# Gathers under way at the phase ends, inputs brought a phase early, and a merge that takes one operand after the other

## The reference

```python
h = rms_norm(x, n_mix_pre) * (1 + sc1) + sh1          # sc, sh, g: from the conditioning vector
bg, cg, hin, q, k, v, r, ga, gb, alow = split(h @ w_in)
branch_a = (bg * conv3(cg * hin)) @ w_proj_a
branch_b = (rms_norm(gated_linear_attention(q, k, v)) * silu(r)) @ w_proj_b
m = (sigmoid(ga) * branch_a + sigmoid(gb) * branch_b) @ w_out
x = x + g1 * rms_norm(m, n_mix_post)
h = rms_norm(x, n_ffn_pre) * (1 + sc2) + sh2
# PEER: 8 heads, each takes the 16 best of 128*128 experts by two sets of 128 sub-keys
s = (h @ wq) . subkeys; top 16 of each half, of the 256 sums the top 16 -> expert, gate = softmax
act = gelu(u_tab[expert] . h)                          # 128 rows of u per token
y = sum(gate * act * v_tab[expert])                    # 128 rows of v per token
x = x + g2 * rms_norm(y, n_ffn_post)
```

## Time and profile before

| | |
|---|---|
| runs | 4400.0, 4410.25, 4410.38 us |
| profiled execution, its own time | 4404.23 us |
| its span | 4402.1 us |
| busy | PE 3206.2 us (73%), DVE 2480.9 (56%), POOL 1645.8 (37%), ACT 804.7 (18%) |
| DMA | 1359.01 MB, mean 309 GB/s; gathers (queue q0) 1140.92 MB, other loads and stores (q1) 215.09 MB |
| part 0's phases | about 695 to 1174 us, gathers from 1080 us |
| part 1's phases | 1174 to 2171 us |
| part 2's phases | 2171 to 3370 us |
| last phase | 3370 to 4402 us |

### The profile page before, as it was taken

One profiled execution on the slowest core, in us unless ns is written; L12 is line 12 of the kernel. 1 busy time (PEld: TensorE's weight loads), 2 busy tenths in 40 slices (PEclk: granted clock), 3 DMA queues, 4 the chain that ended last, 5 costly groups with the idle time before them and its releaser, 6 DMA issues. The chain is left out here.

```text
span 4402.1 us, 46784 instructions
## 1 busy us (share of the span) xinstructions
PE 3206.2 (73%) x15781; PEld 1734.2 (39%) x15781; DVE 2480.9 (56%) x7734; ACT 804.7 (18%) x1299; POOL 1645.8 (37%) x1380
## 2 busy tenths in 40 slices
PE   5999997775597776766688666677665666677676
PEld 2998896754164542431155333144111111111111
DVE  2435554138764546777665554677775555555555
ACT  4223323342123112210014111211000010000000
POOL 2111104524255543543255444354333333333332
PEclk8999998977798986977789888698666666666666
DMA  8011003424799989989899999999899999999998
GB/s 339 26 60 60 31 30 129 127 98 145 292 373 370 364 354 359 378 346 364 322 383 410 360 358 361 384 412 364 356 399 361 412 415 404 411 415 404 415 413 345
DMA packets 225975, 1359.01 MB, mean 309 GB/s; under 512 B 29286, under 2 KB 38406, under 8 KB 83532
## 3 DMA queue, kind: packets, MB, share of 16 engines
q0 software_dynamic: 156672, 1140.92, 64.3%
q1 hardware_dynamic: 69068, 215.09, 13.4%
HBM read 1322.56 MB, written 33.35 MB: 308 GB/s over the span
## 5 line engine op out<-in xcount | busy, mean ns | idle before, releaser
L1083 DVE CUSTOM_DVE_ANT_0 peer_uv<-peer_uv,all_PS 128x512 f32<-128x512 f32 x2176 | 1435.4, 685 | 1140.3 <-PE all_PS L1021 585.5
L1021 PE MATMUL all_PS<-peer_hT,peer_sel 96*128 96x512 bf16 x2176 | 972.8, 463 | 949.3 <-DVE peer_halves L1083 799.0
L1004 POOL DMA_INDIRECT peer_uv<-in_uv,peer_idx x1088 | 1041.5, 957 | 1600.3 <-PE all_PS L1041 1198.8
L1021 PEld LDWEIGHTS all_PS<-peer_hT,peer_sel 96*128 96x128 bf16 x2176 | 205.0, 101 | 1776.3 <-DVE peer_halves L1083 1291.7
L1041 PE MATMUL all_PS<-peer_uv,peer_zw 128*32 128x512 f32 x4352 | 835.0, 869 | 1.5 <-DVE peer_zw L1103 1.5
L888 POOL TENSOR_TENSOR flow_w_lo<-flow_w,flow_w_hi 128x1024 fp32r<-128x1024 f32 (+1 forms) x204 | 460.4, 2262 | 541.1 <-ACT flow_w_hi L881 537.3
L1057 ACT ACTIVATE peer_ge<-peer_pre 128x4 f32<-128x4 f32 x272 | 56.1, 206 | 2121.4 <-DVE peer_pre L1089 1955.9
L1041 PEld LDWEIGHTS all_PS<-peer_uv,peer_zw 128*32 128x32 f32 x4352 | 154.0, 142 | 423.8 <-issue 422.0
L908 PE MATMUL all_PS<-mix_h_hi,flow_w_hi 128*128 128x384 f32 (+1 forms) x672 | 281.7, 419 | 31.6 <-POOL flow_w_lo L888 31.6
L881 ACT ACTIVATE flow_w_hi<-flow_w 128x1024 fp32r<-128x1024 f32 (+1 forms) x204 | 203.6, 1004 | 327.3 <-PE all_PS L910 134.9
L910 PE MATMUL all_PS<-mix_h_hi,flow_w_lo 128*128 128x384 f32 (+1 forms) x672 | 224.6, 334 | 0.0
(11 more groups left out here) (294 smaller groups left out, 4679.6 us busy)
## 6 DMA issues: line engine op xcount, KB each, us to landing
cond_w<-in_w_ada SPq DMA_DIRECT2D x12, 2048.0 KB, 11.8
flow_w<-in_w_gate_ab SPq DMA_DIRECT2D x48, 512.0 KB
flow_w<-in_w_query SPq DMA_DIRECT2D x48, 512.0 KB
flow_w<-in_w_conv SPq DMA_DIRECT2D x36, 512.0 KB
peer_uv<-in_uv,peer_idx POOLq DMA_INDIRECT x1088
gla_w<-in_w_heads SPq DMA_DIRECT2D x24, 512.0 KB, 3.9
flow_w<-in_w_proj_b SPq DMA_DIRECT2D x24, 512.0 KB
flow_w<-in_w_out SPq DMA_DIRECT2D x24, 512.0 KB
```

The costliest lines, as they stand in the source:

```text
L1004: self.nc.gpsimd.indirect_dma_start(out=self.uv[:, n % self.NUV, :], out_offset=None, in_=self.A["uv"], in_offset=bass.IndirectOffsetOnAxi ...
L1021: nc.tensor.matmul(PS[:, f, :], self.sel[:, c:c + 1].broadcast_to([3 * GR, P]), self.hT[:, g % self.NH, f * 512:(f + 1) * 512], start=True ...
L1083: nc.vector.tensor_tensor_reduce(part, part, PS[:, f, :], 1.0, 0.0, ALU.mult, ALU.add, self.halves[:, d, f, e:e + 1]).then_inc(M["dotted"], 1)
```

## The change

- `Gather.fetch` gets a third argument. With it POOL goes on to `upto + 8` (`FULL` = `NUV - 2`) and not to `upto + 4`. Every phase ends with `gat.fetch(pool, hi, True)` behind its loop; in norm and pick that call stands alone for all of POOL's gathers.
- The marks are rounded so that each hi is 2 modulo 4: part 0's pick takes 26 tokens and not 24, part 1 ends at 318 and part 2 at 702 and not at 320 and 704. So the sum of the last full group is issued by the phase's last spread, and of ten buffers eight are free.
- `Early`: tiles on the other side of SBUF that outlive a phase. The h of a part's mix is brought in the middle of the pick before it (`bring_h`); norm's lines, `pick` and x rows are brought in out. The taps and the bias of the convolution are loaded once, for part 0.
- In mix, merge and out ACT and DVE take the gather turns of `before()` first and split afterwards.
- merge takes all eight products of a (4 chunks each) and then all eight of o (8 chunks each), where it took them in turn; the stream of weights is ordered so, too. o is split at steps 3, 4, 5 and 6 of the loop, and the sums of the two come in steps 8 to 15.
- norm's scratch row lies in the tile of the key lists.

```diff
+    FULL = NUV - 2
-    def fetch(self, pool, upto):
+    def fetch(self, pool, upto, full=False):
-        for n in self.steps("pool", upto + self.AHEAD if upto else 0):
+        assert not full or upto in (0, T) or upto % BT == 2
+        for n in self.steps("pool", upto + (self.FULL if full else self.AHEAD) if upto else 0):
...
+class Early:
+    def __init__(self, nc, sems, tag, tiles):
+        self.room = Scope(nc, tag)
+        self.tiles = [self.room.twin(q, shape, "right") if twin else (self.room.sb(q, shape, side="right"), None)
+                      for q, shape, twin in tiles]
+        self.sems = sems
+    def free(self):
+        self.room.tensors.close()
+def bring_h(sp, A, part, brought):
+    for g in range(2):
+        sp.dma_start(brought.tiles[0][0][:, 4 * g:4 * g + 4], A["h1"][part.index, :, 4 * g:4 * g + 4, 0:part.n]).then_inc(brought.sems[g], 16)
...
 # mix_phase
-            h.fetch(sp)
-            for dst, src in ((taps, A["conv_w"]), (cbias, A["conv_b"]), (past, A["conv_state"])):
-                sp.dma_start(dst[:], src).then_inc(small_in, 16)
+            if part.index == 0:
+                bring_h(sp, A, part, brought)
+                for dst, src in ((taps, A["conv_w"]), (cbias, A["conv_b"]), (past, A["conv_state"])):
+                    sp.dma_start(dst[:], src).then_inc(small_in, 16)
+            gat.fetch(pool, hi, True)          # also behind the loops of merge, out and keys; alone in norm and pick
+            gat.gelu(act, turns.before())      # mix, merge and out alike
             h.make_high(nc, act)
-            gat.gelu(act, turns.before())
+            gat.dots(dve, turns.before())
             h.make_low(nc, dve)
-            gat.dots(dve, turns.before())
...
 # merge_phase
+        O_AT = (3, 4, 5, 6)
-                w.product(nc, pe, w0 + j, bank(j), (a, o)[j % 2], lambda k, nk: gat.spread(pe, turns.within(j, k, nk)))
+                w.product(nc, pe, w0 + j, bank(j), (a, o)[j // KD], lambda k, nk: gat.spread(pe, turns.within(j, k, nk)))
-            o.make_high(nc, act)
+                if j in O_AT:
+                    o.make_high(nc, act, O_AT.index(j))
-                d, q = divmod(j, 2)
+                q, d = divmod(j, KD)
...
 # out_phase, SP
+            for q in range(3):
+                sp.dma_start(lines[q * GR:q * GR + NC, :], A["rows"][q]).then_inc(brought.sems[0], 16)
+            sp.dma_start(pick[:, :], A["line_pick"]).then_inc(brought.sems[0], 16)
...
+                if 0 < j <= nt:
+                    i, u = j - 1, part.tiles[j - 1]
+                    sp.dma_start(x[0:part.rows[i], i, :], A["x_rows"][u, 0:part.rows[i], :]).then_inc(brought.sems[1 + i], 16)
...
 # pick_phase, SP
+                if j == NJ // 2 and following:
+                    bring_h(sp, A, following, brought)
...
 # hybrid_decoder
-                        marks = [0, 0, 0, 0, 0, 0, 24]
+                        marks = [0, 0, 0, 0, 0, 0, 26]
-                        span = gat.before[part.tiles[0]] - lo
-                        marks = [lo + span * sum(SHARES[:i]) // sum(SHARES) for i in range(len(SHARES) + 1)]
+                        span = gat.before[part.tiles[0]] - 2 - lo
+                        marks = [lo + span * sum(SHARES[:i]) // sum(SHARES) // BT * BT for i in range(len(SHARES) + 1)]
```

More of the change, by code:

```diff
@@ L916, with __init__ @@
 class Halves:
-    def __init__(self, sc, tag, chunks, n, group, source=None, twin=None):
+    def __init__(self, sc, tag, chunks, n, group, source=None, twin=None, landed=None):
         self.groups, self.group, self.source = chunks // group, group, source
@@ L922, in __init__ @@
         self.hi = sc.sb(f"{tag}_hi", [P, chunks, n], F32R)
-        self.landed = [sc.sem(f"{tag}_in{g}") for g in range(self.groups)] if source else None
+        self.landed = landed or ([sc.sem(f"{tag}_in{g}") for g in range(self.groups)] if source else None)
         self.high, self.low = sc.sem(f"{tag}_high"), sc.sem(f"{tag}_low")
@@ L1149, in mix_phase @@
         PS = G["PS"]
-        h = Halves(sc, "h", KD, n, 4, lambda g: A["h1"][part.index, :, 4 * g:4 * g + 4, 0:n])
+        h = Halves(sc, "h", KD, n, 4, twin=brought.tiles[0], landed=brought.sems)
         NJ, NCONV = 3 * CC + 2 * KD, 3 * CC
@@ L1342, in _ @@
         def _(sp):
+            lines, pick, x = (q for q, _ in brought.tiles)
+            for q in range(3):
+                sp.dma_start(lines[q * GR:q * GR + NC, :], A["rows"][q]).then_inc(brought.sems[0], 16)
+            sp.dma_start(pick[:, :], A["line_pick"]).then_inc(brought.sems[0], 16)
             gat.turn(sp, turns.before())
@@ L1383, in _ @@
         def _(act):
+            gat.gelu(act, turns.before())
             x.make_high(nc, act)
-            gat.gelu(act, turns.before())
             for j in range(NJ):
@@ L1396, in _, with norm_phase @@
         def _(dve):
+            gat.dots(dve, turns.before())
             x.make_low(nc, dve)
-            gat.dots(dve, turns.before())
             for j in range(NJ):
                 gat.dots(dve, turns.upto(j))
-def norm_phase(nc, A, G, part, gat, m_rows, h, lo, hi):
+def norm_phase(nc, A, G, part, gat, m_rows, brought, junk, h, lo, hi):
     with Scope(nc, f"norm{part.index}") as sc:
@@ L1407, in norm_phase @@
         R = part.rows
-        x = sc.sb("x", [P, nt, D])
-        lines, pick = sc.sb("lines", [3 * GR, D]), sc.sb("pick", [3 * GR, P + TAIL])
-        junk = sc.sb("junk", [P, D])
+        lines, pick, x = (q for q, _ in brought.tiles)
+        lines_in, x_in = brought.sems[0], brought.sems[1:]
         ss, root = sc.sb("ss", [P, 2, nt]), sc.sb("root", [P, 2, nt])
         assert not part.samples or part.index == 0
-        lines_in, row_mm, squared, logged, rooted, gated, x2_done, gained, h2_done, t_mm, high = (sc.sem(q) for q in (
-            "lines_in row_mm squared logged rooted gated x2_done gained h2_done t_mm high").split())
-        x_in, x2_saved = ([sc.sem(f"{q}{i}") for i in range(nt)] for q in ("x_in", "x2_saved"))
+        row_mm, squared, logged, rooted, gated, x2_done, gained, h2_done, t_mm, high = (sc.sem(q) for q in (
+            "row_mm squared logged rooted gated x2_done gained h2_done t_mm high").split())
+        x2_saved = [sc.sem(f"x2_saved{i}") for i in range(nt)]
         block = sc.block()
@@ L1426, in _ @@
         def _(sp):
[L1427 to L1431, removed]
             gat.turn(sp, turns.before())
@@ L1441, in _ @@
         def _(pool):
-            gat.fetch(pool, turns.before())
-            for j in range(NJ):
-                gat.fetch(pool, turns.upto(j))
+            gat.fetch(pool, hi, True)
         @block.tensor
@@ L1703, in lows, with pick_phase @@
         return 2 * self.tiles
[L1706 removed]
+def pick_phase(nc, A, G, part, gat, best, place, following, brought, lo, hi):
     with Scope(nc, f"pick{part.index}") as sc:
@@ L1734, in _ @@
                 gat.turn(sp, upto(j))
+                if j == NJ // 2 and following:
+                    bring_h(sp, A, following, brought)
         @block.gpsimd
         def _(pool):
-            for j in range(NJ):
-                if j >= early:
-                    gat.fetch(pool, upto(j))
+            gat.fetch(pool, hi, True)
         @block.tensor
@@ L2015, in hybrid_decoder @@
                     with Scope(nc, f"mid{part.index}") as mid:
-                        spare = mid.sb("spare", [P, len(part.tiles) * D])[:, :]
+                        nt = len(part.tiles)
+                        spare = mid.sb("spare", [P, nt * D])[:, :]
                         m_rows = spare.rearrange("p (t d) -> p t d", d=D)
+                        norm_in = [mid.sem(f"norm_in{i}") for i in range(nt + 1)]
                         with Scope(nc, f"join{part.index}") as join:
```

70 lines of the change are left out of this document (44 added, 26 removed).

## The result

| | before | after |
|---|---|---|
| median (lowest to highest), us | 4407.39 (4400.0 to 4410.38), 4 runs | 4511.85 (4510.58 to 4517.03), 4 runs |
| profiled execution's span, us | 4402.1 | 4510.0 |
| ratio after / before | | 1.0242, 95% interval 1.0224 to 1.0260 |

The kernel became 104 us slower; 4504 was forecast. The page's DMA slices after, to hold against the earlier trace rows: many nines of the parts' stretches have become eights, and one a six; those of the last phase stand.

The account below looks back on a forecast made before the run. DMA was taken as the bound: bytes over 411 GB/s plus its idle time at the barriers. 4404.2 + 97 - 4 = 4497 for the profiled execution, 6 us under the runs' median, so 4504; range 4430 to 4550 us.

Parts of the forecast that it names:

- POOL's drain waits for landing; the barrier for the drain: Phase ends: POOL's drain returns only once its gathers landed; the last four gathers add 10.2 us to it.
- rival A: Drain not held by the landing, so eight gathers run through the barrier: faster, about -75, 4335 us; chance 10%.
- No buffer free until the first sum: Behind the barriers: eight buffers full, no gather until the next sum; idle 153.8 us against 56.4, cost 97 us.
- Idle ahead stays: Ahead of the barriers: DMA idle time from the last packet to the open barrier stays, only shifted by the longer queue.
- a DMA share above 0.8 ahead of the barriers: Sign of the forecast: no engine busy for some 20 us before each barrier while DMA share there rises above 0.8.
- Part 0, -4: Part 0, without gathers: norm and merge starts lose short waits, between 0 and 8 us, 4 taken as gain.
- Marks, 0 (-3 to +3): Rounded marks, smaller tiles and taps loaded once: taken as 0, bounds -3 and +3.
- Order of merge, 0 (-5 to +25): Merge, all of a then all of o: up to 3 us in 8 steps of two merges; 0 taken, bounds -5 to +25.
- cross-check: Counting engine time: 13 barriers each open 10.2 us later, 133, less 38 given back at the starts: +95.
- Starts: Phase starts in the check by engine time: merge 2 x 7, mix 2 x 5, norm 2 x 7, 38 us given back.
- Rival B: No difference: +56 behind barriers, up to 45 us regained later in the phases by eight tokens in hand; 4417, chance 8%.
- Rival C: Slower still: second group of four late in mix and keys, merge's o half bound by PE; +25 to +45, 4540; chance 12%.

Follow-up runs that it names:

- experiment 1: Changed kernel with POOL's fetch at a phase's end reaching 0, 4 or 6 tokens beyond hi, where it was 8: 4446.94, 4392.04 and 4454.47 us.
- (3): Six phases' barriers of semaphores alone, no POOL drain: changed kernel 4310.36 us, with fetch to hi + 4 only 4319.46 us; kernel before 4347.18 us.
- experiment 5: Kernel before with only the rounded marks, gathers to hi + 4 at the ends as before: 4418.96 us, ratio 1.0045.
- open barriers: Changed kernel with the barriers at the six phases' ends made of semaphores alone and POOL not draining there: 4310.36 us, ratio 0.9804.
- experiment 4: Changed kernel without POOL's drain at the six phases' ends: merge in turn again 4325.69 us; splitting ahead of the gather turns again 4308.48 us.
- Experiment 2: Kernel before with only the rounded marks and the fetch to hi + 8 at the phase ends: 4547.02 us, ratio 1.0343.

## Why the prediction was right

By its own steps:

- **POOL's drain waits for landing; the barrier for the drain.** Right: 2.8 us for each gather more (experiment 1), gone with the drain (3), and the drains end 1.5 to 4.4 us behind the last gather packet. What rival A took for its condition, a drain that the landing does not hold, is not what happened.
- **No buffer free until the first sum.** Right: 148 us idle behind the barriers, 154 forecast; +92 over the kernel before, +97 forecast. By phase, both parts, in us idle of 30 (forecast, part 1, part 2): mix 16.8, 18.9, 16.8; merge 11.2, 10.8, 9.3; out 15.9, 11.4, 5.4; norm 11.1, 15.6, 15.9; keys 5.9, 8.4, 6.3; pick 11.1, 11.1, 10.5; last 9.8, 7.2. Out and norm were each off, to opposite sides. The x rows, 1.5 MB, now come in out's first steps and fill part of its gap (they land in a median of 11.9 us in part 1 and 6.2 in part 2); I had counted them as moved but not in that gap. Why part 2's gap is shorter by another 6 us stays open. The first product on DVE was to come within 2 us of each barrier; it does at eleven of the 13, but in norm the tokens do not start at 1.2 us: PE spreads a row line first, 3.75 us, and the first product on DVE comes 5.1 us behind the barrier at 1651.1:

```profile
1651.73 3.75 PE L1482 MATMUL all_PS<-early_lines,early_pick 9*128 9x512 f32 x4 [22.78 <-PEq L111]
...
1656.17 0.69 DVE L1086 CUSTOM_DVE_ANT_0 peer_uv<-peer_uv,all_PS 128x512 f32<-128x512 f32 x1 [28.49 <-PE all_PS L1024]
```

- **Idle ahead stays.** Right: 67.7 and 68.0. But the sign named for it, a DMA share above 0.8 ahead of the barriers, did not come: 68 us of 13 times 20 is a share of 0.74, after as before. That sign did not fit the prediction's own sum, which left this idle time where it was.
- **Part 0, -4.** Its phases up to pick took 353.4 us and not 361.9, so -8.5, just past the bound of 8. A further -8.4 us lies in the first stretch, which the change doesn't touch; over all runs that stretch ends anywhere from 682 to 694 us.
- **Marks, 0 (-3 to +3).** Wrong by size: +20 us alone (experiment 5). This is most of the +33 in "rest": part 1's pick has 30.6 us idle in its middle against 10.7, part 2's 13.8 against 5.3. Missed because I looked at marks as counts of tokens and not at where in a group of four they fall.
- **Order of merge, 0 (-5 to +25).** About -13 with open barriers (experiment 4), outside the bounds on the side of gain.
- **Starts.** The cross-check gave 38 us back for them. Experiment 2 says 35 to 44 for all that is not marks or queue, but some 13 of that is the order of merge, and taking the tokens before the split was worth nothing in experiment 4. By this reckoning the starts brought less than 38, how much no run shows, and that the two roads agreed was partly luck.
- **Slips in the sums.** Mix's gather comes out at 19.2 and not 19.4 us, which changes the forecast by less than 1 us. Half of B's 45 us takes the low end from 4462 to 4440 and not to 4430.

The sum came out close partly by chance. In the profiled execution it is +92 where 97 stood, then +33 unforeseen and -17 where -4 stood, of which half lies in the first stretch, where the runs scatter by as much.

Rival A fell in experiments 1 and 3. Rival B fell with idle time in mid-phase that grew by 33 us where it was to shrink by up to 45. Rival C's starvation did not come (idle behind and rest are accounted for without it), nor a loss in merge.

## What to carry to other kernels

Before filling a queue ahead of a barrier, ask what the barrier waits for: if the issuing engine drains, its transfers must land, and what counts then is how many buffers are free when it opens. The best of the four numbers tried was the one that keeps DMA busy through the drain and leaves half the buffers, four of eight here. Better still was to take POOL's drain out: 52 us in the kernel before, some 200 in the one after. A shift of the marks by two tokens was not free here (some 20 us); that a turn list which repeats every few steps keeps a bad place for a whole phase is the likely reason, not a shown one.

## What the runs showed of the hardware

The recorded length of a drain is no measure of what it waits for: with four gathers ahead its median was 10.2 us in the kernel before, and with the rounded marks alone 15.4 us, with the same 11 us from the last product on DVE to the open barrier. The record begins when POOL's sequencer comes to the drain: in the kernel before that lies between 2.4 us ahead of the end of POOL's last gather instruction and 11.1 us behind it, over the 13 phase ends. Its end is what follows the landing. The prediction's "10.2 us is four gathers" was a fit by luck: the drain did wait for the gathers, but its length did not say so. The distance from the last product on DVE to the open barrier (table of experiment 1) is the better measure.
